# Two layers of a hybrid diffusion block on one core: the pace of the expert gathers set per run, and the second layer's modulation moved

## The reference, cut to what matters

```python
mod = silu(c) @ w_mod + b_mod                     # 6 vectors of 1024, for latents and for context
h = modulate(rms_norm(x, g1), mod[0], mod[1])
q, k, v, cq, ckv, kr, uv, gate = split(h @ w_in)
a = neighbourhood_attention(q, k, v, context k, v, relative bias)   # context: plain attention
m = latent_attention(cq, ckv, kr)                 # low-rank queries and keys, rotary part
s = spatial_gating(uv)
x = x + mod[2] * ((sig(g_a)*(a@Wa) + sig(g_s)*(s@Ws) + sig(g_m)*(m@Wm)) @ w_out)
h2 = modulate(rms_norm(x, g2), mod[3], mod[4])
# expert layer: 8 heads x 16 experts of 16384 for each token, chosen by two top-16 lists
idx, gate = product_key_topk(h2 @ w_q)
act = gelu(sum_d exp_u[idx] * h2)                 # one row of 1024 for each token and expert
x = x + mod[5] * sum_k gate * act * exp_v[idx]    # and another row
```

## Time and profile before

| engine | busy us | share |
|---|---|---|
| PE (TensorE matmul) | 4447.6 | 79% |
| DVE (VectorE) | 3051.5 | 54% |
| POOL (GpSimd, issues gathers) | 2763.0 | 49% |
| ACT (ScalarE) | 1241.3 | 22% |

### The profile page before, as it was taken

How to read it: one execution, slowest core, us unless ns; L and a number is a source line. 1 busy time by engine, 2 the same in 40 slices (tenths; PEclk the granted TensorE clock), 3 DMA queues, 4 the chain that set the end, 5 groups by cost and what they waited for, 6 DMA issues and landing times.

```text
span 5613.4 us, 57357 instructions
## 1 busy us (share of the span) xinstructions
PE 4447.6 (79%) x19168; PEld 2455.9 (44%) x19168; DVE 3051.5 (54%) x8176; ACT 1241.3 (22%) x3643; POOL 2763.0 (49%) x2566
## 2 busy tenths in 40 slices
PE   7989798889997887997855558999788889655555
PEld 4467643433585344653411115558533455311111
DVE  0211767776217776556676542431677655777643
ACT  1321222333212321112211112540133211111111
POOL 0000466666304655666677770000366466777776
PEclk9889898888998888998977888999888999877778
DMA  5544799988747878999999992114688799999999
GB/s 189 189 153 142 282 367 340 335 311 331 253 137 279 324 286 304 379 398 358 356 390 369 394 389 83 55 39 154 221 310 318 278 366 399 391 391 391 362 403 353
DMA packets 464130, 1651.73 MB, mean 294 GB/s; under 512 B 51168, under 2 KB 57440, under 8 KB 463840
## 3 DMA queue, kind: packets, MB, share of 16 engines
q0 software_dynamic: 368640, 1342.34, 63.2%
q1 hardware_dynamic: 95200, 305.73, 15.2%
HBM read 1645.77 MB, written 2.10 MB: 294 GB/s over the span
## 4 chain that ended last, share of the span: by engine, by line
PE 50%; POOL 15%; DVE 13%; DMA 11%; issue 7%; ACT 3%; SPq 0%; DVEq 0%; POOLq 0%; ACTq 0%; PEldq 0%
PE banks L647 16%; PE banks L925 10%; DMA vb<-in_peer_v_dram,idx 8%; POOL vb L1446 8%; POOL ub L1435 7%; DVE ub L1386 5%; PE banks L736 4%; PE banks L663 3%; PE banks L773 3%; PE banks L835 3%; PE banks L812 2%; PE banks L758 2%; PE banks L823 1%; DMA ub<-in_peer_u_dram,idx 1%; PE banks L715 1%
## 5 line engine op out<-in xcount | busy, mean ns | idle before, releaser
L1435 POOL DMA_INDIRECT ub<-in_peer_u_dram,idx x1280 | 1424.1, 1113 | 2270.7 <-DVE idx L1374 1375.1
L925 PE MATMUL banks<-vb,dg 128*64 128x512 f32 x5120 | 1571.7, 741 | 695.7 <-DMA vb<-in_peer_v_dram,idx 626.4
L1386 DVE CUSTOM_DVE_ANT_0 ub<-ub,h2cur 128x1024 f32<-128x1024 f32 x1280 | 1529.6, 1223 | 611.1 <-DMA ub<-in_peer_u_dram,idx 485.9
L1446 POOL DMA_INDIRECT vb<-in_peer_v_dram,idx x1280 | 1338.3, 1046 | 561.0 <-issue 342.5
L925 PEld LDWEIGHTS banks<-vb,dg 128*64 128x64 f32 x5120 | 406.7, 160 | 1596.1 <-issue 1336.4
L647 PE MATMUL banks<-region,wring 128*128 128x256 f32 x3840 | 882.2, 390 | 35.8 <-ACT region L989 25.3
L647 PEld LDWEIGHTS banks<-region,wring 128*128 128x128 f32 x3840 | 738.7, 195 | 215.8 <-issue 104.9
L1135 ACT ACTIVATE dg<-consts,wgt 128x64 f32<-128x64 f32 x1280 | 358.4, 337 | 836.5 <-PE banks L925 425.3
L647 PE MATMUL banks<-h2T,wring 128*128 128x256 f32 x1280 | 316.9, 406 | 21.1 <-ACT h2T L989 21.1
L1329 DVE SCALAR_TENSOR_TENSOR region<-region,banks 128x256 f32<-128x256 f32 x120 | 50.5, 421 | 486.0 <-PE banks L647 485.9
L736 PE MATMUL banks<-region,wring 128*128 128x256 f32 (+1 forms) x1056 | 260.7, 404 | 48.0 <-ACT region L989 48.0
(11 more groups left out here) (146 smaller groups left out, 4004.9 us busy)
## 6 DMA issues: line engine op xcount, KB each, us to landing
wring<-w_gate_dram SPq DMA_DIRECT2D x120, 512.0 KB, 5.0
wring<-w_mod_dram SPq DMA_DIRECT2D x96, 512.0 KB, 4.6
wring<-w_pq_dram SPq DMA_DIRECT2D x80, 512.0 KB, 5.4
wring<-w_branch_dram SPq DMA_DIRECT2D x60, 512.0 KB, 3.6
wring<-w_out_dram SPq DMA_DIRECT2D x40, 512.0 KB, 4.7
ub<-in_peer_u_dram,idx POOLq DMA_INDIRECT x1280, 6.6
vb<-in_peer_v_dram,idx POOLq DMA_INDIRECT x1280, 6.6
region<-in_na_rpb_dram SPq DMA_DIRECT2D x64, 256.0 KB, 3.0
```

What stands on the lines that cost most here:

```text
L925: ins = nc.tensor.matmul(bank(ACC[a])[64 * g:64 * g + 64, :], dg[:, n % DG_RING, :], vb[:, n % V_RING, a * 512:(a + 1) * 512], start=first ...
L1386: nc.vector.tensor_tensor_reduce(out=ub[:, n % U_RING, :], in0=ub[:, n % U_RING, :], in1=h2cur[:, g, :], scale=1.0, scalar=0.0, op0=ALU.mu ...
L1435: pool.indirect_dma_start(ub[:, n % U_RING, :], None, u_rows, bass.IndirectOffsetOnAxis(ap=idx[:, u % IDX_RING, j:j + 1], axis=0)).then_in ...
L1446: pool.indirect_dma_start(vb[:, n % V_RING, :], None, v_rows, bass.IndirectOffsetOnAxis(ap=idx[:, u % IDX_RING, j:j + 1], axis=0)).then_in ...
```

## The change

- **Pace.** `BG_STEP` is gone. `schedule(steps)` builds the plan twice. The first pass puts in no background work and records the foreground cost at marks: in each query stage after its second score step, at its end, and twice ahead of layer 1's segment B. The second pass uses one step cost per stretch between marks: 4.3 in query stages (`QUERY_STEP`), and elsewhere the value by which `RUN = 120` background steps fit between two query stages' marks. The values come out as 6.29 (layer 0 from C's query to A's query), 3.83 (A's query to B's query), 1.12 (after B's query, layer 1's C keys and A keys), 4.99 (layer 1 up to A's query, where no pairs are left to place), and 3.47 (layer 1, A's query to B's query).
- **Modulation.** The 24 chunks of layer 1 now stand in layer 0's merge of B, two after each second channel. Layer 0's remaining 16 stay where they were: 4 in C's keys stage, 12 in C's attention.
- **Form of a chunk.** `modt` of a chunk now stands ahead of `modr` of the next in the plan, and not behind it. One `modrow` buffer serves all chunks of a layer, in place of two. The matmuls of `modr` write two rows per column group and not 32, so that ScalarE copies four pieces of 2x256 in place of one of 128x256. `cT` and `cS` have storage of their own, for which `IDX_RING` goes from 22 to 21. Layer 1's `modrow` lies in `region`.
- **Names.** Steps of C's keys stage in layer 0 carry one more field (`again`). Layer 1's C keys stage uses another buffer for its norm. Neither adds an instruction.

The pairs (steps `dots`) that the plan puts into each stage, and the chunks:

| stage | pairs before | pairs now | chunks before | chunks now |
|---|---|---|---|---|
| layer 0 C attention / latent / merge | 0 | 0 | 19 / 10 / 7 | 12 / 0 / 0 |
| layer 0 C query | 13 | 13 | | |
| A keys, B keys | 18, 15 | 11, 11 | | |
| neighbourhood A and B | 41 | 27 | | |
| A latent | 37 | 25 | | |
| A merge | 4 (15 sums) | 30 | | |
| A query | 13 (2 sums) | 16 | | |
| B latent | 40 | 43 | | |
| B merge | 44 | 59 | 0 | 24 |
| B query | 18 | 18 | | |
| layer 1 C keys and A keys, to the end of layer 0's pairs | 141 (152 sums) | 131 (142 sums) | | |
| layer 1 B keys to A merge | 0 | 0 | | |
| layer 1 A query | 13 (2 sums) | 13 (2 sums) | | |
| layer 1 B latent | 40 | 47 | | |
| layer 1 B merge | 44 | 54 | | |
| layer 1 B query | 18 | 19 | | |
| after it | 141 (152 sums) | 123 (134 sums) | | |

The diff, cut to its core:

```diff
-U_RING, V_RING, IDX_RING, DG_RING = 6, 6, 22, 8
+U_RING, V_RING, IDX_RING, DG_RING = 6, 6, 21, 8
-BG_STEP = 4.2
+RUN, QUERY_STEP = 120, 4.3
...
         def emit(step, cost=0.0):
             plan.append(step)
-            owed[0] += cost
-            while owed[0] >= BG_STEP:
-                owed[0] -= BG_STEP
+            pace["cost"] += cost
+            if pace["steps"] is None or not pace["marks"]:
+                return
+            step_cost = pace["steps"][len(pace["marks"]) - 1]
+            pace["owed"] += cost
+            while pace["owed"] >= step_cost:
+                pace["owed"] -= step_cost
                 if not bg_step():
-                    owed[0] = 0.0
+                    pace["owed"] = 0.0
+        def mark():
+            pace["marks"].append(pace["cost"])
...
                     for hf in range(2):
                         add_load((l, "mod", c, hf), w_mod[l, c, hf])
-                    emit(("modr", l, c), 1.2)
                     if c not in (0, 8):
                         emit(("modt", l, c - 1), 0.4)
+                    emit(("modr", l, c), 1.2)
...
+        def layer_tail(l, s):
+            mla_stage(l, s)
             fence()
+            if l == 0 and s == B_S:
+                mods.extend((1, c) for c in range(24))
+            merge_stage(l, s)
+            query_stage(l, s)
+            fence()
...
+        schedule(None)
+        marks = pace["marks"] + [pace["cost"]]
+        steps = []
+        for n in range(0, len(marks) - 1, 2):
+            here, query_end, run_end = (marks + marks[-1:])[n:n + 3]
+            steps += [QUERY_STEP, (run_end - query_end) / (RUN - (query_end - here) / QUERY_STEP) + 1e-3]
+        schedule(steps)
...
-                            ins = nc.tensor.matmul(bk[32 * g:32 * g + 32, 0:256], cS[:, k, :], w[:, g * 256:(g + 1) * 256],
+                            ins = nc.tensor.matmul(bk[32 * g:32 * g + 2, 0:256], cS[:, k, :], w[:, g * 256:(g + 1) * 256],
...
-                    if cnt["mod"] >= 2:
-                        whole(act, mod_keys[-2])
-                    frees(nc.scalar.activation(modrow[:, cnt["mod"] % 2, :], bk[:, 0:256], ACT.Copy), key)
+                    if mod_keys:
+                        whole(act, mod_keys[-1])
+                    if n == 0:
+                        link(nc.scalar.activation(modrow_of[l], consts[:, 0:N], ACT.Copy, scale=0.0))
+                    for g in range(4):
+                        rows = slice(32 * g, 32 * g + 2)
+                        ins = nc.scalar.activation(modrow_of[l][rows, :], bk[rows, 0:256], ACT.Copy)
+                    frees(ins, key)
```

More of the change, by code:

```diff
@@ L375, in kq_stage @@
             t0 = N * s
-            emit(("norm", l, s, "kq"), 6.0)
+            again = 1 if l == 0 and s == CTX_S and queries else 0
+            emit(("norm", l, s, "kq" if s or queries else "kc"), 6.0)
             emit(("h_wait", "kq"))
@@ L522, in query_stage @@
         def query_stage(l, s):
-            assert not mods or l or s
+            assert not [m for m in mods if m[0] == l]
             if bgs["avail"]:
@@ L570, in program, with schedule @@
-        while bg_step():
-            pass
+            mark()
+        def layer_tail(l, s):
+            mla_stage(l, s)
+            fence()
+            if l == 0 and s == B_S:
[3 more added lines that the diff above has]
+            fence()
+        def schedule(steps):
+            for a in (plan, loads, pace["marks"], bias_order, mods):
+                a.clear()
+            for a in (load_at, batches, units_of, bsb_no):
+                a.clear()
+            fences[0] = 0
+            pace.update(owed=0.0, cost=0.0, steps=steps)
+            bgs.update(avail=0, front=0, d=0, g=0, a=0, rate=1)
+            mods.extend((0, c) for c in range(8))
+            some_mods(8)
+            mods.extend((0, c) for c in range(8, 24))
+            for l in range(LAYERS):
+                if l:
+                    until_tail(tile_no[(0, 1)])
+                kq_stage(l, CTX_S, l == 0)
+                fence()
+                if l == 0:
+                    na_stage(0, (CTX_S,))
+                    fence()
+                    layer_tail(0, CTX_S)
+                for s in (A_S, B_S):
+                    if l:
+                        if s == B_S:
+                            mark()
+                        until_tail(tile_no[(0, 2 * s + 1)])
+                        if s == B_S:
+                            mark()
+                    kq_stage(l, s, True)
+                    fence()
+                na_stage(l, (A_S, B_S))
+                fence()
+                layer_tail(l, A_S)
+                layer_tail(l, B_S)
+            while steps is not None and bg_step():
+                pass
```

98 lines of the change are left out of this document (35 added, 63 removed).

## The result

The changed kernel took 5660.02 us (median of 4 runs, 5659.14 to 5669.49) against 5602.56 us for the kernel before on the same chip. The ratio is 1.0104, with a 95% interval of 1.0087 to 1.0122. It is 1.0% slower, where 1.1% faster was forecast. The span of its profiled execution is 5667.7 us, 54.3 us more than before.

The account below looks back on a forecast made before the run. DMA was taken to bound the drains; in mixed stages neither PE nor DMA was full. −38 − 56 + 129 − 56 − 42 = −63 us gave a median of 5542 us, 1.1% faster, with 8 in 10 from 5470 to 5620.

Parts of the forecast that it names:

- The first stretch: Layer 0 from C's query to A's query: −56 us, from neighbourhood −50, latent −31, A's merge +54, keys −29.
- smoothing alone gives little: Foreground stages: a pair moved between them is worth almost nothing; gain comes only as more pairs leave the drains.
- the −52 of the sum: C's attention and merge: moving modulation out saves 17 chunks × 1.54 = 26 and 7 × 3.75 = 26 us.
- the new form at +14 us: Chunks in the start and C's keys stage: waiting for ScalarE's copies costs +11 and +3 us.
- bring it nearer to 1, so I take 470: B's merge, layer 0: more bytes for the same PE work raise the DMA share from 0.89; 470 us, +120.
- its sign of failure: The forecast fails if layer 0's B merge exceeds 510 us, or the neighbourhood stage does not shrink by 40 us.
- The prices by addition: B's merge, layer 0: 349.8 + 15 × 3.4 + 24 × 3.75 gives 491 us.
- the rule on round-robin queues: DMA engines alternate between queues, so weights get about half of 395 GB/s and layer 0's B merge lies near 447 us.
- pairs at 3.4 us and the query at +4: Layer 1: B's merge gains 10 pairs at 3.4 us, +34, with +32 taken; one more in B's query, +4.
- price in full: Rival, no change: dense merges are bound by bytes, so a pair costs as in a drain; median 5609 us, chance 0.18.
- The line for the twins: Layer 1 stages without pairs against layer 0's with them; the merge of 44 pairs gives 3.4 us a pair.
- its own ends (447 to 527): B's merge, layer 0, by bytes: 447 us at 395 GB/s, 527 at 335.

Follow-up runs that it names:

- old_order: The changed kernel with `modr` ahead of the `modt` of the chunk before and two `modrow` buffers, two rows and four copies kept; ratio 1.0046 at 5600.
- one_copy: The changed kernel with 32 rows per column group and one copy of 128x256, keeping the new order and one buffer; ratio 0.9977 at 5840.
- pace_only_3: The kernel before with the new pace alone, chunks and their form as before; ratio 0.9976 where the kernel before took 5604 us.
- light_chunks: The changed kernel with the old form of a chunk, loads of layer 1's chunks cut to 64 of 1024 columns; ratio 0.9967 at 5600.
- border: The pace alone with 3.85 in place of 3.47 in layer 1's last stretch, putting a tile border behind B's query; ratio 0.9847 against 0.9868.
- first_run: The kernel before with one background step per 6.3 of cost from C's query to A's query, 4.2 elsewhere; ratio 0.9955 at 5600.

## Why the prediction was wrong

**Where it held.** The drains: −55 and −101 us measured against −56 and −98. B's latent: +8 against +9. The first stretch: −76 against −56, with the neighbourhood stage giving 63 and not 50, the latent 21.5 and not 31, and A's merge costing 39 and not 54. The start: 4.53 us a chunk against 4.4. The words that smoothing alone gives little came true at 5600 (0.9976, −13 us), but not by the prediction's prices: by them the pace alone was worth −99 us. And the move's gain ahead of the gathers is in part luck: with the old order and four copies the first query norm stands 48 us earlier than before, against the −52 of the sum, but the 17 chunks of attention and latent gave 10 us and not 26, and the seven of the merge 34 and not 26.

**C's attention: a clock that the sum did not have.** The sum had the new form at +14 us, all of it ahead of C's attention, and the chunks there at 1.54 us, a row taken at the higher clock. The stage took 18 us more and not 11 less. (The kernel before took 62.6 to 68.8 us there in its three profiles.) old_order and one_copy show the cause: with `modt` ahead of `modr`, the clock stays at 0.50, which is the lower of its two levels, 1.2 GHz, for all of the stage, and with the old order it rises within it (0.73 to 0.84 on average). PE is busy in the window in both, 77.8 of 80.5 us and 57.0 of 58.5. By the busy time alone one could not have told them apart. Busy time times clock is nearly the same, 77.8 × 0.50 = 38.9 and 57.0 × 0.73 = 41.6, so the clock accounts for the whole difference.

**B's merge in layer 0: the step "bring it nearer to 1, so I take 470".** It took 511 us by the table's borders, +167 and not +120, and by the prediction's own windows 518.8, over the 510 that it had named as its sign of failure. Its DMA share stayed at 0.90 and 341 GB/s, against 0.89 and 335 before. Bytes and waits added up in place of overlapping. The prices by addition (15 × 3.4 + 24 × 3.75 = +141) were nearer. pace_only_3 shows what the first ten pairs cost without a chunk, 49 us and not 34, and light_chunks shows that only 41 us of the 88 to 108 for the chunks are their bytes, so a floor by bytes was the wrong end to lean on. By the rule on round-robin queues (the Trainium skill, DMA: Bandwidth & Descriptors, section on queues, rings and completion order) the merge should have come near 447 us; the measured 511 decides against that use of it, since TensorE waits for chunk loads all the same (38.6 us). A share of the bandwidth does not say how late one load is: in light_chunks TensorE waited 29.3 us for loads with a sixteenth of the bytes.

**Layer 1: pairs at 3.4 us and the query at +4.** B's latent, merge and query took 105 us more for 18 pairs, and not 56: 31 for 7 pairs, 48 for 10, and 25 in the query for one. So a pair moved into a dense stage costs 4.4 to 4.8 us, near the drain's 5.5, and the tile border that came along into the query stage costs 25 more, as border shows. Where the price of a pair in the merge comes from can be read from the sums on TensorE, 4350.2 to 4690.9 us before and 4431.7 to 4820.9 now (busy us, mean ns, then idle before them and what ended it):

```profile
L925 PE MATMUL banks<-vb,dg 128*64 128x512 f32 x348 | 88.7, 632 | 5.2 <-DMA vb<-in_peer_v_dram,idx 4.1 <-ACT dg L1135 1.1
```

```profile
L958 PE MATMUL banks<-vb,dg 128*64 128x512 f32 x432 | 114.7, 654 | 31.0 <-DMA vb<-in_peer_v_dram,idx 23.6 <-ACT dg L1172 7.0 <-ACTq L633 0.4
```

Ten pairs more are 26 us of sums and 26 us of waits ahead of them, 20 of these for `v` rows that had not landed; waits for the top-k fell by 5 us. The sum had taken the mean of a merge in which these rows were waited for during 4 us. For this layer that is near the price of the rival "price in full", whose chance was 0.18, but its reason, merges bound by bytes at the drain's rate, isn't shown: where a drain runs at 352 GB/s and not 383, the merge of B in layer 0 took 391 and 393 us with the pace alone, and 392.6 here. Its time for the whole, 5609 us, missed the form. The mean price of a pair over a stage, 3.4 us, was not the price of the next pair. The line for the twins holds 44 pairs at once, and at 54 the curve is steeper.

**Smaller.** C's query and A's query of layer 1 are 12 and 8 us longer, the first since the debt of cost starts at zero; the second has the same longer wait, with its cause untried. The sum had nothing for either.

Together, against the −63 us of the sum: attention and form +26, C's query +12, the first stretch −20, B's merge +47, layer 1 +51. That makes +53, and the two spans differ by +54. The sign was lost by three terms. B's merge lay inside its own ends (447 to 527) but above the value taken. Layer 1 as a whole (+9 against −64 to −4) and the part ahead of the gathers (−12 against −38) were priced by means and by a clock that did not hold for what was moved. (One slip of addition in A's merge, 198.9 + 30 × 2.9 = 286 and not 287, changes nothing.)

At 5600 the best ratio is that of first_run, one changed pace in one stretch: 0.9955 against 0.9976 for the pace alone. Their intervals overlap, so that it is the better of the two isn't shown.

## What to carry to other kernels

A twin stage gives the mean price of background work, and the next piece costs more: over 44 pairs the mean was 3.4 us, and the next ten cost 4.8 us each, which is nearly what the work cost where nothing was beside it (5.5). Before moving work between such stages, count how many pieces leave the stretch where only they run, and price those alone. When a producer's step is put right ahead of its own consumer's, look at what the engine clock did in that stage, not only at busy time.

## What the runs showed of the hardware that I had not expected

- TensorE can be busy for 97% of a stage and be granted 0.50 throughout (77.8 of 80.5 us, C's attention as changed), while the same instructions in another order were granted 0.73 (57.0 of 58.5 us).
- A ScalarE copy of 2x256 takes 374 ns as the median, about as long as one of 128x256 (383 ns); four in a row take 1.53 us.
- Weight loads of 32 KB, issued beside gathers, landed after 5.6 us in the median, and TensorE still waited 29.3 us for 48 of them (58.7 us with 512 KB each).
- The same kernel took 5600 us in some sets of runs and 5830 to 5850 in others, on one chip 5829 and later 5601. Gathers ran at 352 GB/s in the drain there and not 383, and the ratio of this change moved from 1.0104 to 0.9995 and 1.0005.
